# One pack of modulation columns moved to GpSimd and ScalarE, and another order around the attention units

## The reference

```
mx = split(silu(c) @ w_mod[l] + b_mod[l], 9)       # for the 256 tokens of x
mz = split(silu(c_ctx) @ w_mod[l] + b_mod[l], 9)   # for the 256 context tokens z
x = x + 0.5 * mx[2] * swiglu(modulate(rms_norm(x), mx[0], mx[1]), ffn1...)   # z alike with mz
hx = modulate(rms_norm(x), mx[3], mx[4]) @ w_in[l]                            # hz alike
mix = concat(fourier, neighborhood attention, gated linear attention, grouped attention)
x = x + mx[5] * (mix_x @ w_out[l])
x = x + 0.5 * mx[8] * swiglu(modulate(rms_norm(x), mx[6], mx[7]), ffn2...)
```

## Time and profile before

| what | us |
|---|---|
| median of 3 runs | 3266.78 (3264.37 to 3268.36) |
| profiled execution | 3264.09 |
| its span, first to last instruction | 3262.3 |
| PE busy | 3210.9 |
| DVE busy | 2051.9 |
| ACT busy | 618.3 |
| POOL busy | 89.9 |

### The profile page before, as it was taken

How to read it: one execution, slowest core, us unless ns; L and a number is a source line. 1 busy time by engine, 2 the same in 40 slices (tenths; PEclk the granted TensorE clock), 3 DMA queues, 4 the chain that set the end, 5 groups by cost and what they waited for, 6 DMA issues and landing times. The chain is left out here.

```text
span 3262.3 us, 44573 instructions
## 1 busy us (share of the span) xinstructions
PE 3210.9 (98%) x17268; PEld 2705.4 (83%) x17268; DVE 2051.9 (63%) x4140; ACT 618.3 (19%) x1354; POOL 89.9 (3%) x158
## 2 busy tenths in 40 slices
PE   8999999999999999999999989999999999999999
PEld 7888888988888889888884645888888888765899
DVE  6678757667787677664654763655656556455576
ACT  2121112121211122100013361000010000234221
POOL 0000000000000000000000100000000000001000
PEclk9999999999999999999999999999999999999999
DMA  6744677556356885332324242432324323325563
GB/s 193 186 119 143 235 227 227 183 155 168 104 161 230 234 234 179 104 116 65 93 76 119 42 150 77 106 104 78 98 72 105 102 78 103 99 84 123 140 176 132
DMA packets 597249, 442.00 MB, mean 135 GB/s; under 512 B 27072, under 2 KB 586592, under 8 KB 596656
## 3 DMA queue, kind: packets, MB, share of 16 engines
q1 hardware_dynamic: 583264, 392.53, 41.4%
q0 software_dynamic: 12304, 44.94, 4.7%
q10 hardware_dynamic: 1472, 1.68, 0.2%
HBM read 438.06 MB, written 1.05 MB: 135 GB/s over the span
## 5 line engine op out<-in xcount | busy, mean ns | idle before, releaser
L2156 PE MATMUL psum<-hh,ring 128*128 128x256 f32 (+1 forms) x4608 | 1074.0, 392 | 3.6 <-DVE hh L1654 3.0
L2156 PEld LDWEIGHTS psum<-hh,ring 128*128 128x128 f32 x4608 | 872.1, 190 | 180.9 <-issue 70.1
L2384 PE MATMUL psum<-hh,arena 128*128 128x256 f32 x1056 | 249.5, 379 | 0.0
L2384 PE MATMUL psum<-hh,ring 128*128 128x256 f32 x1056 | 242.1, 381 | 1.9 <-ACT hh L1424 1.9
L2384 PE MATMUL psum<-arena 128*128 128x256 f32 x1056 | 238.7, 379 | 0.0
L1725 DVE SCALAR_TENSOR_TENSOR arena<-arena,par 128x255 f32<-128x255 f32 (+14 forms) x480 | 225.3, 469 | 17.0
L2407 PE MATMUL psum<-arena 128*128 128x256 f32 x1056 | 231.8, 379 | 0.0
L2384 PEld LDWEIGHTS psum<-hh,ring 128*128 128x128 f32 x1056 | 198.6, 190 | 35.2 <-ACT hh L1424 4.9
L2384 PEld LDWEIGHTS psum<-hh,arena 128*128 128x128 f32 x1056 | 200.6, 190 | 27.3
L2384 PEld LDWEIGHTS psum<-arena 128*128 128x128 f32 x1056 | 200.6, 190 | 27.3
L2407 PEld LDWEIGHTS psum<-arena 128*128 128x128 f32 x1056 | 200.6, 190 | 27.3
(11 more groups left out here) (309 smaller groups left out, 3660.9 us busy)
## 6 DMA issues: line engine op xcount, KB each, us to landing
ring<-in_ffn_w SPq DMA_DIRECT2D x176, 512.0 KB, 5.2
ring<-in_w_in SPq DMA_DIRECT2D x54, 1024.0 KB, 5.3
ring<-in_w_up SPq DMA_DIRECT2D x88, 512.0 KB, 5.7
ring<-in_w_in SPq DMA_DIRECT2D x84, 512.0 KB, 5.2
mod_rows<-in_w_mod_rows POOLq DMA_DIRECT2D x72, 512.0 KB, 3.9
ring<-in_w_mod_late SPq DMA_DIRECT2D x36, 1024.0 KB, 5.1
ring<-in_ffn_w SPq DMA_DIRECT2D x16, 1536.0 KB, 6.6
ring<-in_ffn_w SPq DMA_DIRECT2D x16, 1280.0 KB, 5.8
```

What stands on the lines that cost most here:

```text
L2156: ins = mm(o[0:rows_, 0:T], w[:, k, c0:c0 + rows_], src[:, k, 0:T], start=(k == 0), stop=(k == kt - 1))
L2384: ins = mm(o[:, 0:S], lhs[:, k, :], rhs[:, k, :], start=(k == 0), stop=(k == half - 1))
```

## The change

It does six things.

1. The middle pack of layer 1's modulation (pieces 12 to 23 of 36) is no longer a product of PE. In the two feed-forwards of layer 0, once for `c` and once for `c_ctx` (`w`), GpSimd loads 24 tiles of 128 transposed rows of `w_mod[1]` one after another into the two buffers, multiplies each by the row of silu(c) in place (`modw`), and ACT copies the product onto itself with its sum as a second output (`moda`). Part 0 loads the row (`mod_r`); parts 1 to 24 have a multiply, parts 2 to 25 a sum. DVE adds bias and 1 at the end (`mod_w`).
2. The remaining 24 pieces are dealt anew: five in layer 0's attention loop, none in layer 1's. The seven-bank ring therefore lasts until after layer 1's projections.
3. The scores and maxima of a unit are a step of their own (`at_s`); those of units 0 and 1 are issued ahead of and behind the GLA norm, and the flips follow them. Their banks are held back while the flips take theirs.
4. The first three output tiles begin among the last units (`out_front`: six of the eight products, with their banks held), and end (`out`: the products of tiles 2 and 3) after the loop.
5. The gate groups (`g_d`, `g_w`) come one or two units earlier; the bias load waits for the first transform (`four1`) instead of the second.
6. In layer 1 a value step stands ahead of the transform, a rotation comes one projection later and the level steps alternate with three fillers instead of two; in layer 0 an exponential part is ahead of the context GLA output.

The core of the diff:

```
+def row_turn(p, s):
+    if 0 < p.rows <= 2 * PACK:
+        p.step("moda", DEPTH - 1, 2 * PACK + p.rows - 1, s)
+        if p.rows == 2 * PACK and s:
+            p.step("mod_w", DEPTH - 1)
+    if p.rows < 2 * PACK:
+        p.step("modw", DEPTH - 1, 2 * PACK + p.rows, s)
+    p.rows += 1
...
+        if p.pieces == PIECES + PACK:
+            p.pieces += PACK
...
     if last:
-        return [0, 1, 0, 1, 0, 1, 0, 1, 1, 1, 1, 0]
-    return [0, 1, 0, 1, 0, 1, 0, 1, 0, 1, 0, 1, 0, 1, 0, 1, 1, 1, 0, 0]
+        return [0, 0, 0, 0, 0, 0, 0, 0, 0, 0, 0, 0]
+    return [0, 0, 1, 1, 1, 0, 0, 1, 0, 0, 0, 1, 0, 0, 0, 0, 0, 0, 0, 0]
...
             if e == 2:
                 mod_turn(p)
+            if l == 0:
+                if e == 0:
+                    p.rows = 0
+                    p.step("mod_r", l, w)
+                else:
+                    row_turn(p, w)
...
-        if 2 <= n and order[n - 2] >= 4:
+        m = n - 3 if last else n - 2
+        if m >= 0 and order[m] >= 4:
...
     if last:
         fourier_in(0)
         fourier_in(1)
+        value(0)
         for part in (1, 2):
             p.step("g_mul", l, 0, part)
         fourier_rows(0)
-        value(0)
         value(1)
         gla_keys()
         fourier_cols(0)
         p.step("na_load", l)
         gla_state()
-        gla_scores(0, lambda: value(2), lambda: value(3))
-        gate_r(0)
-        flips()
+        gla_scores(0, lambda: value(2), lambda: value(3), lambda: gate_r(0))
         gate_r(1)
...
+        p.step("g_exp", l, 0, 1)
         gla_out(1)
-        p.step("g_exp", l, 0, 1)
         p.step("g_mul", l, 0, 0)
         p.step("g_exp", l, 0, 2)
+        p.step("na_load", l)
         fourier_cols(1)
-        p.step("na_load", l)
...
     gla_out(0)
+    scores(0)
+    for b in range(2):
+        p.hold("at", l, 0, b)
     gla_norm(0)
+    scores(1)
+    for b in range(2):
+        p.hold("at", l, 1, b)
+    flips()
...
-    scale_at = {5: (0, 0), 7: (0, 1)} if last else {13: (0, 0), 15: (0, 1)}
+    scale_at = {4: (0, 0), 6: (0, 1)} if last else {11: (0, 0), 13: (0, 1)}
...
+        if len(units) - 1 <= n <= len(units):
+            out_front(n - len(units) + 1)
         if 2 <= n < len(units) + 2:
             p.step("at_t", l, n - 2)
...
+        if n == len(units) + 1:
+            out_front(2)
...  # GpSimd
+                elif kind == "mod_r":
+                    w = r[0]
+                    if w == 0:
+                        pool.wait_ge(row_summed, COLUMN_STEPS)
+                    else:
+                        pool.wait_ge(late_row_summed, 2 * PACK)
+                        produced(pool, job[("out", 0, KT - 1)])
+                    pool.dma_start(late_row, bass.AP(tensor=c_src.tensor, offset=w * D, ap=[[0, P], [1, D]])).then_inc(late_row_in, 16)
+                    load_late_rows(w, 0)
+                    load_late_rows(w, 1)
+                elif kind == "modw":
+                    n, w = r[0] - 2 * PACK, r[1]
+                    if n == 0:
+                        pool.wait_ge(late_row_ready, w + 1)
+                    if 1 <= n < 2 * PACK - 1:
+                        pool.wait_ge(late_row_summed, 2 * PACK * w + n)
+                        load_late_rows(w, n + 1)
+                    pool.wait_ge(late_rows_in[n % 2], 16 * (PACK * w + n // 2 + 1))
+                    buf = row_buf[:, n % 2, :]
+                    nc.gpsimd.tensor_tensor(buf, buf, late_row, ALU.mult).then_inc(late_row_done, 1)
...  # ScalarE
+                elif kind == "moda":
+                    f, w = r
+                    n = f - 2 * PACK
+                    act.wait_ge(late_row_done, 2 * PACK * w + n + 1)
+                    buf = row_buf[:, n % 2, :]
+                    do(nc.scalar.activation(buf, buf, ACT.Copy, accum_out=mod[:, l, f, w:w + 1]),
+                       late_row_summed, 2 * PACK * w + n + 1)
```

More of the change, by code:

```diff
@@ L181, in __init__ @@
         self.columns = 0
+        self.rows = 0
         self.steps = []
@@ L205, in job @@
             b = self.next_bank % self.ring
+            while b in self.held:
+                b = (b + 1) % self.ring
             self.place.append((b, self.uses[b]))
@@ L212, in job, with hold, release @@
             self.last_job[chunk] = self.number[name]
+    def hold(self, *name):
+        self.held.add(self.place[self.number[name]][0])
+    def release(self, *name):
+        self.held.discard(self.place[self.number[name]][0])
     def load_early(self, chunk):
@@ L508, in plan_second @@
             p.job("nss", l, n - 1)
-        if 2 <= n and order[n - 2] >= 4:
-            p.step("nrot", l, n - 2, order[n - 2])
-            p.job("nrot", l, n - 2)
+        m = n - 3 if last else n - 2
+        if m >= 0 and order[m] >= 4:
+            p.step("nrot", l, m, order[m])
+            p.job("nrot", l, m)
     mod_turn(p)
@@ L549, in gla_level, with gla_scores @@
             p.job("g_lv", l, s, hd, lp)
-    def gla_scores(s, one, two):
+    def gla_scores(s, one, two, three=None):
         p.step("g_x", l, s)
@@ L557, in gla_scores @@
         gla_level(s, 1)
+        if three:
+            two()
         gla_level(s, 2)
-        two()
+        (three or two)()
         gla_level(s, 3)
@@ L635, in plan_second, with scores, out_front @@
         p.step("g_w", l, 1, 1)
+    units = mix_units(last)
+    def scores(n):
+        p.step("at_s", l, n)
+        for b in range(2):
+            p.job("at", l, n, b)
+    def out_front(i):
+        p.step("out_front", l, i)
+        p.job("out_front", l, i, chunk=("out", l, i // 2))
+        p.hold("out_front", l, i)
     gla_out(0)
+    scores(0)
+    for b in range(2):
+        p.hold("at", l, 0, b)
     gla_norm(0)
-    units = mix_units(last)
-    scale_at = {5: (0, 0), 7: (0, 1)} if last else {13: (0, 0), 15: (0, 1)}
+    scores(1)
+    for b in range(2):
+        p.hold("at", l, 1, b)
+    flips()
+    for n in range(2):
+        for b in range(2):
+            p.release("at", l, n, b)
+    scale_at = {4: (0, 0), 6: (0, 1)} if last else {11: (0, 0), 13: (0, 1)}
     for n in range(len(units) + 4):
         if n < len(units):
+            if n >= 2:
+                scores(n)
             p.step("at", l, n)
-            for b in range(2):
-                p.job("at", l, n, b)
         if n in scale_at:
@@ L663, in plan_second @@
         p.step("out", l, i)
-        p.job("out", l, i, chunk=("out", l, i // 2))
+        if i < FRONTS:
+            p.job("out", l, i, chunk=("out", l, i // 2), on=("out_front", l, i))
+            p.release("out_front", l, i)
+        else:
+            p.job("out", l, i, chunk=("out", l, i // 2))
     if last:
@@ L2605, in _ @@
                     w = arrived(("out", l, i // 2))
-                    o = begin(job[("out", l, i)])
-                    order = (0, 1, 4, 5, 6, 7, 2, 3)
+                    front, rest = (0, 1, 6, 7, 4, 5), (2, 3)
+                    if kind == "out_front":
+                        o, order = begin(job[("out_front", l, i)]), front
+                    elif i < FRONTS:
+                        o, order = bank(job[("out", l, i)]), rest
+                    else:
+                        o, order = begin(job[("out", l, i)]), front + rest
                     for k in order:
-                        if i == 0 and k == 4:
+                        if kind == "out_front" and i == 0 and k == 4:
                             pe.wait_ge(gla_ready, gla_count(l, True))
-                        if i == 0 and k in (2, 3):
+                        if kind == "out_front" and i == 0 and k == 6:
+                            evacuated(pe, job[("at_o", l, n // 2 - 3)])
+                        if kind == "out" and i == 0:
                             evacuated(pe, job[("at_o", l, n // 2 - (2 if k == 2 else 1))])
```

37 lines of the change are left out of this document (30 added, 7 removed).

## The result

The changed kernel takes 3241.79 us (median of 4 runs, 3241.54 to 3242.52) against 3265.69 of the kernel before beside it: a ratio of 0.9926, 95% interval [0.9909, 0.9943]. Forecast were 3238 and 3228 to 3254.

The account below looks back on a forecast made before the run. TensorE, busy 98% of 3262.3 us, was taken as the bound; -10.4 - 9.1 - 8.1 - 1.3 - 0.4 + 1.0 = -28.3 us from 3264.09, plus 2.7 to the runs' median, gave 3238, range 3228 to 3254.

Parts of the forecast that it names:

- rival B: Attention loops: DVE sets the pace and the pieces were only filler; gain 17 us, giving 3250; chance 0.19.
- 4, fronts of the layers: Ahead of the attentions: Fourier, rotation and level waits go in layer 1, -8.1 us; layer 0's GLA product wait shrinks, -1.3.
- 2, layer 1's attention: Layer 1's attention, flips counted in: 74.4 us becomes 64.0 with 2.4 idle, -10.4 us (bounds -12.8 and -3.0).
- 3, layer 0's attention: Layer 0's attention, flips and their DMA wait counted in: 123.35 us becomes 114.3, -9.1 us (bounds -14.5 and -3.5).
- the sign that I had set: Each attention stretch: PE idle plus slow clock under 6 us would show the forecast right.
- 1, "at best all of it is span; at worst it turns into waits": Both attentions: twelve modulation pieces leave PE, 12.8 us of matmuls, plus one transpose taken as 0.4; worst case 0.
- 5, the new work: Layer 0's feed-forwards: 48 GpSimd multiplies of 2.6 us and ACT sums of 1.25 add +1.0 us (bounds 0 and +6).
- Rival C: Feed-forwards: multiplies starve DVE, deciding from 4.8 us a part; +82 us, about 3320; chance 0.05.

Follow-up runs that it names:

- e_l1front: Changed kernel with layer 1's order ahead of the attention (value step, rotations, level-step fillers) as before; 3251.43 us.
- e_double: Changed kernel with each of the 48 GpSimd multiplies done twice in place; 3267.73 us, ratio 1.0004 to the kernel before.
- v3: Changed kernel plus one line: unit 2's scores take unit 0's banks instead of unit 1's, in both layers; 3235.71 us, ratio 0.9902.
- e_order: Changed kernel with the middle pack back on TensorE as 12 pieces and nothing on GpSimd, new order kept; 3242.92 us, ratio 0.9924.
- e_nowork: Changed kernel with each multiply and each sum cut to one column, loads and waits kept; 3240.47 us, ratio 0.9915.
- e_offload: Kernel before, its order kept, with only the offload: five pieces in layer 0's attention, none in layer 1's; 3272.15 us, ratio 1.0011.
- e_load: Changed kernel with the bias load back behind the second transform in layer 0, flips staying late; 3240.14 us.

## Why the prediction was right, and where it was not

The total is 3.8 us off, inside the range: the sum had -28.3 us, and -23.9 were measured. The range held rival B's 3250 as well, so that the total is right does not say that the mechanism was. By the prediction's own steps:

- **4, fronts of the layers: right.** Layer 1 -8.1 forecast; -8.9 from before to after (from its first norm to the end of the GLA outputs, flips aside), 10.8 when undone alone. From before to after, the excess is the first level product's wait of 0.61 us and a DMA wait of 0.29, which I had left out. In e_l1front it is clock that fell behind the rotation's wait too (granted 0.50 there; before it stayed 1.00 behind the same 2.47 us). Layer 0: the product's wait went from 1.89 to 1.04 us, -0.85 for -1.3.
- **2, layer 1's attention: right in size.** From the end of the GLA outputs, flips counted in, 74.5 became 63.9: -10.6 for -10.4. The waits are 2.6 us for the 2.4 kept, but elsewhere: 1.91 of them is unit 2's bank, none stands behind the gate group.
- **3, layer 0's attention: the term that was mis-sized.** -5.0 measured (123.4 to 118.4) for -9.1. I had kept 5.5 us idle: 1.3 at the start, 0.9 over the context units, 3.3 at the gate groups. Measured: 1.91 + 1.08 at the start, 0.66 + 0.52 + 0.30 + 0.81 = 2.3 at the context units, 2.10 behind a gate group: 7.4, and 2.6 us of half clock behind the start (PE busy 127.78, against 125.14 in e_double with the clock kept). That also fails the sign that I had set, idle and slow clock under 6 us in each attention stretch. The start is a bank chosen by the plan's turn, which no view of before can show, but the diff can: two pairs of banks are held while the flips take theirs. I read the order of the steps and not the banks. v3 undoes it and gives 3.55 back.
- **1, "at best all of it is span; at worst it turns into waits".** The sum took the removed matmuls in full and put the waits beside them. That came out as a number and is misleading as a cause: with the new order in place the pieces are worth 3.6 us in layer 1 and next to nothing in layer 0, and the order by itself has the ratio 0.9924, that of the whole change (0.9926). That the total still came out is luck in this respect: the order with the pieces left in was better than I had priced it. Rival B had the mechanism in the main (the idle time rose by 3.2 and 2.7 us where the pieces went), but not the banks; its 3250 was too high because its 17 us held only waits that the profile of before named. The order with the pieces, e_order, gained 25.7 us. It also has the pieces at other turns than before; how much of the gain is theirs no run shows.
- **5, the new work: right.** +1.0 forecast; the arithmetic alone is 0.54 + 0.52 = 1.06 (e_nowork), and loads and waits add 0.3 in the first feed-forward (530.23 against 529.93). Multiply 2.40 us on the mean (median 2.36) for 2.6, sum 1.24 for 1.25. The rule of the Trainium skill that I had weighed (SBUF — State Buffer, "Who interferes with whom": exclusion for a whole instruction, issue order decides) holds as to exclusion, also in the direction that no row of before showed: DVE is held 3.26 us for 0.69. As to the order the trace does not plainly agree: the held record starts 0.32 us *ahead* of the multiply. By the Trainium skill, GPSIMD Engine Reference, "Elementwise — side-by-side cycle accounting", I had an estimate of 2.2 us; the trace's median is 7% more.
- **Rival C** was real in kind, with a wrong way of counting. Two multiplies are 2.37 + 2.58 = 4.95 us a part; 48 parts at 0.15 over C's 4.8 would be 7 us, and 26 came. The bill is not paid part by part: DVE falls behind by some 0.4 us a part, 4.0 us by the first turn, and PE pays when the sums are due, and again where the last multiplies stand back to back. Between 2.4 us (1.1 us of cost) and 4.95 the point was not located.

That e_offload lost 1.6 us ahead of the context norm is clock: behind the same 1.89 us wait for the first GLA product the granted clock was 0.58 and 0.57 over the next 4 us, and 1.00 before. It cost nothing in the end, since before PE waited 2.45 us for the bias there; the flips start at 1882.45 and 1882.57 us.

Not settled: what lets the clock fall behind a wait in one execution and keeps it in another, and what e_offload would take with its first piece in a free bank.

## What to carry to other kernels

Work of the bounding engine that stands in front of another engine's result is filler, and its removal is worth only what the order around it lets through: measure it with the order of before *and* after (here -3.5, -0.7 to 1.6 and 5.2 to 6.3 us for the same 12.8 us of matmuls). Removing it can also shift the turn of the PSUM banks, as it did here twice. Where a change holds or moves banks, follow the turn by hand and look whose last reader each new product meets. Work added on an engine that excludes another is not safe by the held engine's mean load alone: DVE busy 9.0 and 10.7 of 12.1 us a part cost 0.5 us in a feed-forward, 11.3 cost 12.5, and the price was paid at a turn between stages and where the added work came in a burst.

## What the runs showed of the chip

The same code with the same waits ran at two clocks. Six microseconds behind the 1.91 us wait of unit 2, in e_l1front, in the changed kernel and in e_double (the column before the DMA share is PE's granted clock):

```profile
1900.78:1906.78 6.00, 5.04 (x28) 2.74 (x28) 2.68 (x6) 2.75 (x6) 0.00 (x0) 0.50 0.01 3
```

```profile
1902.44:1908.44 6.00, 4.92 (x28) 2.50 (x28) 2.68 (x6) 2.75 (x6) 0.00 (x0) 0.55 0.01 3
```

```profile
1914.80:1920.80 6.00, 4.30 (x38) 2.48 (x36) 3.31 (x7) 2.75 (x6) 0.00 (x0) 1.00 0.09 18
```

In the first two PE is at 1.2 GHz nearly throughout, in the third at 2.4. There is a second such place, the wait of 2.10 us behind the second gate group. Two microseconds behind it, in e_nowork and in the changed kernel:

```profile
1944.30:1946.30 2.00, 2.00 (x10) 0.81 (x8) 1.46 (x5) 1.90 (x6) 0.00 (x0) 0.50 0.01 4
1947.00:1949.00 2.00, 2.00 (x12) 0.81 (x9) 1.65 (x5) 1.90 (x6) 0.00 (x0) 1.00 0.02 4
```

The two places account for the spread of attention 0 in five executions of equal code there: 135.08 us with the clock kept at both (e_double), 136.70 where it fell at the gate group (e_nowork), 136.95 and 137.13 where it fell at the start (e_load and the changed kernel), 138.71 where it fell at both (e_l1front). So a fall costs 1.6 to 2.0 us here on top of the wait, and whether it comes differs from execution to execution. A wait whose cure is worth 2 us by the profile may be worth twice that.

PE and ACT felt nothing of the exclusion between DVE and GpSimd: 12.10 us a part and 0.63 us a Silu, as before, though DVE was held in every part.
